# Routing the second tile of tokens first in a product-key expert layer, with its gathered rows fetched and multiplied between the pieces of the first tile's routing, and six row buffers

## The chip, the core and the metric

The kernel runs on one core of a Trainium2 chip. The core has five engines that run side by side: TensorE (PE; PEld is its weight load), VectorE (DVE), ScalarE (ACT), GpSimd (POOL) and SyncE (SP), each with an instruction queue of its own, and 16 DMA engines that all queues share. They wait for each other by semaphores. Data is worked on in the on-chip memory (SBUF, 128 partitions) and matmuls write to PSUM, eight banks. The metric is the device time of one execution in microseconds (us).

## What is computed

The program is a trunk of two layers over 256 tokens of 1024 numbers each: a mixer (matrix-memory LSTM in layer 0, differential attention in layer 1) and, after each, an expert feed-forward with 16,384 experts per layer. The change is in the feed-forward, of which this is the reference, cut:

```python
def peer_ffn(x, norm_g, w_query, sub_keys, u_table, v_table):
    h = rmsnorm(x, norm_g).reshape(T, D)                       # T = 256, D = 1024
    q = (h @ w_query).reshape(T, PEER_HEADS, 2, PEER_DHALF)    # 8 heads, two halves
    s = jnp.einsum('thpd,hpnd->thpn', q, sub_keys)             # 128 keys a half
    vals, idx = lax.top_k(s, PEER_TOPK)                        # 16 best of each half
    cand = vals[:, :, 0, :, None] + vals[:, :, 1, None, :]
    cidx = idx[:, :, 0, :, None] * N_KEYS + idx[:, :, 1, None, :]
    top_s, pos = lax.top_k(cand.reshape(T, PEER_HEADS, 256), PEER_TOPK)
    experts = jnp.take_along_axis(cidx.reshape(T, PEER_HEADS, 256), pos, axis=-1)
    gates = jax.nn.softmax(top_s, axis=-1)
    ...
        act = jax.nn.gelu(jnp.einsum('td,ted->te', hb, u_table[eb]))
        return jnp.einsum('te,ted->td', gb * act, v_table[eb])
```

So a token picks 8 x 16 = 128 experts; each has a row of u, with which the token's hidden vector is multiplied, and a row of v, which is added with the gate times the gelu of that product.

## The kernel before

All tables are float32. The feed-forward of a layer (`ffn(l)` on every engine) treats its 256 tokens in two ways.

**160 tokens (`N`) go through the whole table.** The table streams in as **units** of 512 KB: 128 up units (a unit is all 1024 numbers of 128 experts of u) and 128 down units of v. SP loads them into a ring of four buffers (`raw`, `RING`, L447), each as soon as the unit four before it is used. TensorE multiplies an up unit with the hidden vectors `h32` in 8 matmuls (`up`, L1751; the trace has 16 records a unit) and ScalarE writes the gelu to `G` (L770), two units at a time. VectorE multiplies `G` with the gates: for groups of 8 tokens it makes one-hot matrices (`one_hots`, L1276 to L1286), TensorE turns them into a 128 x 64 table of gates (`weights`, L1762) and VectorE multiplies (`weigh`, L1296); that happens from unit 64 (`HALF`) to 104 and from 128 to 168. The down units (`down`, L1811) then sum over the experts.

**The other 96 tokens are "own" tokens**, the last ones of the second tile of 128 tokens (`GT` = 64 and `GT2` = 32). Their rows are gathered: GpSimd issues an indirect DMA (`fetch`, L543) that brings 128 rows of 4 KB, one in each partition, 512 KB in all. There are 96 fetches of u rows and 96 of v rows in a layer (`FETCHES`), into a ring of four buffers (`FETCH_RING`, `fetched`). A u fetch is multiplied with the own hidden vectors on VectorE (`row_dot`, L1316, called a dot here), a v fetch is added into `own_out` (`row_add`, L1324). GpSimd issues fetch n when dot or addition n - 4 is done. VectorE goes through the units by number (the loop over `w` from `DOT_AT` = 48, `wait_ge(used, first + w)`), and `row_unit(k)` says at which unit dot or addition k stands: from unit 48 to unit 248 (`ADDED_AT`), with a gap of `GELU_GAP` units between the two kinds.

**The routing** is the top-k search, and VectorE does it by itself beside the first up units. It comes in pieces. A first-level piece (`top16`, L1182 to L1194, over 128 keys) searches four of the 16 score rows of a tile: four pieces a tile, eight in all. GpSimd then makes 80 candidate sums a head (`candidates`, L497), and a second-level piece searches four heads: two pieces a tile. The differences of the best scores go to ScalarE for the exponential (L763, at unit `EXP_AT` = 32). The rank arithmetic (L1222 to L1233) turns places among the candidates into ranks, the expansion (L1237 to L1246, once for each tile and half) turns ranks into key numbers, and L1247 makes the expert number. After the softmax (L1250 to L1252) VectorE signals `slots_ready` and `own_ready` (L1255). GpSimd spreads the expert numbers and gates of the own tokens over the partitions by six small DMAs (`own_indices`, L533) and can issue its first fetch. TensorE transposes the key numbers and gates (`slots`, L1772) ahead of unit 44 (`SLOTS_AT`), and VectorE copies them out (L1260 to L1265) and makes the first two one-hots ahead of the dots.

The order of work on an engine is the order of the code; there is no scheduler. Most of the buffers named are areas of one tensor `big` (`area`), laid out by hand so that areas which are dead by then lie over each other. `G` takes its first 20,480 columns.

## Time and profile before

| | |
|---|---|
| median of 3 runs | 1674.6 us (1673.51 to 1674.79) |
| the profiled execution | 1676.3 us, span 1674.5 us |
| TensorE busy | 1609.0 us, 96% of the span |
| VectorE busy | 1086.8 us, 65% |
| DMA | 531.89 MB, mean 318 GB/s; 241 to 410 GB/s in the slices of the feed-forward |
| the chain that ended last | TensorE 73%, DMA 20% |
| up and down matmuls | 609.4 us (L1811) and 583.1 us (L1751), 4096 records each |

The two feed-forwards are the stretches from 194 to 832 us and from 1027 to 1665 us. A busy TensorE is not a TensorE at its peak, since the ends of matmuls are modelled in the trace. What it waits for is seen better in how far apart the units stand. The granted TensorE clock is 1.00 in all the stretches shown below. In the rows by stretch, the busy time of each engine is in us, with the number of its instructions in brackets; the last three columns are the granted TensorE clock, the busy share of the DMA engines, and what they moved.

### The profile page before, as it was taken

Reading aid. Unit: us, or ns where it says so; the run is one execution under the profiler, and the core shown is the slowest. Engines: PE = TensorE matmul, PEld = TensorE weight load, DVE = VectorE, ACT = ScalarE, POOL = GpSimd, SP = SyncE. Lnnn points to the kernel's source line nnn. Section 1 sums busy time; section 2 is a strip of 40 time slices with the busy share of each in tenths; the row PEclk is TensorE's granted clock in tenths of the full one; section 3 lists DMA queues with packets and bytes.
Section 4 is the critical chain, followed back from the end, with each engine's and each line's share of the span. In section 5 each row is a group of like instructions: output and inputs, shape, how many; then the busy total and the mean of one; then the engine's idle time right before and its main releaser. Section 6 shows DMA issues by size and latency. Waiting matters only on the chain.

```text
span 1674.5 us, 30593 instructions
## 1 busy us (share of the span) xinstructions
PE 1609.0 (96%) x11542; PEld 1466.0 (88%) x11542; DVE 1086.8 (65%) x2275; ACT 296.5 (18%) x632; POOL 434.2 (26%) x457
## 2 busy tenths in 40 slices
PE   8999999999999999999999999999999999999999
PEld 6788999899988988888877789998999899888887
DVE  5588795478747864544278777954787487654552
ACT  5485411000000000000056752110000000000000
POOL 0012001234433343333000020013344332433330
PEclk9999999999999999999999999999999999999999
DMA  6546478999999999999754264789999999999995
GB/s 244 161 136 197 151 241 279 355 393 410 409 409 399 352 404 409 409 409 410 275 165 140 100 205 140 246 279 362 391 408 408 409 403 358 409 409 410 409 410 193
DMA packets 149137, 531.89 MB, mean 318 GB/s; under 512 B 16880, under 2 KB 20224, under 8 KB 148672
## 3 DMA queue, kind: packets, MB, share of 16 engines
q1 hardware_dynamic: 88416, 321.43, 51.8%
q0 software_dynamic: 56672, 204.70, 31.5%
q10 hardware_dynamic: 3968, 4.71, 1.2%
q8 instruction: 48, 0.79, 0.2%
q14 instruction: 33, 0.27, 0.0%
HBM read 527.41 MB, written 1.06 MB: 316 GB/s over the span
## 4 chain that ended last, share of the span: by engine, by line
PE 73%; DMA 20%; issue 3%; DVE 3%; ACT 1%; ACTq 0%; SPq 0%; POOL 0%; DVEq 0%
PE ps L1811 30%; PE ps L1751 21%; DMA raw<-stream 17%; PE ps L1567 4%; PE ps L1582 3%; DMA big<-u_rows,own 3%; PE ps L1584 3%; PE ps L1583 3%; PE ps L1565 2%; PE ps L1762 2%; PE ps L1739 1%; PE ps L1702 1%; PE ps L1922 1%; PE ps L1564 1%; PE ps L1892 0%
## 5 line engine op out<-in xcount | busy, mean ns | idle before, releaser
L1811 PE MATMUL ps<-big,raw 128*128 (+1 forms) x4096 | 609.4, 304 | 26.6 <-DMA raw<-stream 6.7
L1811 PEld LDWEIGHTS ps<-big,raw 128*128 128x128 f32 x4096 | 562.0, 190 | 70.8 <-issue 62.9
L1751 PE MATMUL ps<-big,raw 128*128 128x160 f32 x4096 | 583.1, 301 | 17.7 <-DMA raw<-stream 14.5
L1751 PEld LDWEIGHTS ps<-big,raw 128*128 128x128 f32 x4096 | 559.3, 190 | 36.8 <-DMA raw<-stream 18.5
L1324 DVE SCALAR_TENSOR_TENSOR big<-big,own_act 128x1024 f32<-128x1024 f32 x192 | 246.6, 1285 | 213.9 <-DMA big<-v_rows,own 209.7
L1316 DVE SCALAR_TENSOR_TENSOR big<-big 128x1024 f32<-128x1024 f32 x192 | 233.7, 1224 | 151.9 <-DMA big<-u_rows,own 104.5
L543 POOL DMA_INDIRECT big<-u_rows,own x192 | 198.8, 1035 | 335.2 <-DVE big L1316 319.2
L543 POOL DMA_INDIRECT big<-v_rows,own x192 | 193.0, 1005 | 321.5 <-DVE big L1324 305.3
L575 ACT ACTIVATE wh<-raw 128x1024 fp32r<-128x1024 f32 x97 | 102.1, 1058 | 311.1 <-DMA raw<-stream 275.6
L895 DVE TENSOR_TENSOR wl<-raw,wh 128x1024 fp32r<-128x1024 f32 x97 | 122.1, 1269 | 49.2 <-ACT wh L575 27.4
L770 ACT ACTIVATE big<-ps 128x320 f32<-128x320 f32 x128 | 56.0, 437 | 552.4 <-PE ps L1751 513.1
L1567 PE MATMUL ps<-hT,wh 128*128 128x512 f32 x280 | 100.2, 396 | 0.0
L1582 PE MATMUL ps<-wh,hT 128*128 128x512 f32 x224 | 91.5, 408 | 0.1
L1583 PE MATMUL ps<-wl,hT 128*128 128x512 f32 x224 | 87.9, 392 | 0.0
L1584 PE MATMUL ps<-wh,hT 128*128 128x512 f32 x224 | 87.9, 392 | 0.0
L1565 PE MATMUL ps<-hT,wl 128*128 128x256 f32 x320 | 83.0, 280 | 0.0
L1296 DVE SCALAR_TENSOR_TENSOR big<-ps,big 128x512 f32<-128x512 f32 x80 | 54.9, 686 | 17.3 <-PE ps L1762 13.5
L1565 PEld LDWEIGHTS ps<-hT,wl 128*128 128x128 f32 x320 | 60.3, 188 | 4.3
L1567 PEld LDWEIGHTS ps<-hT,wh 128*128 128x128 f32 x280 | 52.6, 188 | 10.3
L522 POOL DMA_DIRECT2D big<-big x12 | 6.3, 538 | 211.9 <-DVE big L888 211.9
L1281 DVE TENSOR_TENSOR hots_i<-iota_h,slot_d 128x1024 f16<-128x1024 f16 x80 | 54.8, 685 | 0.0
L1286 DVE TENSOR_TENSOR hots_j<-same_j,gate_d 128x1024 f16<-128x1024 f16 x80 | 54.8, 685 | 0.0
(250 smaller groups left out, 1057.4 us busy)
## 6 DMA issues: line engine op xcount, KB each, us to landing
raw<-stream SPq DMA_DIRECT2D x609, 512.0 KB
big<-u_rows,own POOLq DMA_INDIRECT x192
big<-v_rows,own POOLq DMA_INDIRECT x192
big<-keys ACTq DMA_DIRECT2D x2, 1024.0 KB, 7.6
big<-row_copy ACTq DMA_DIRECT2D x6, 256.0 KB, 5.4
x<-x_in SPq DMA_DIRECT2D x1, 1024.0 KB, 5.8
big<-big POOLq DMA_DIRECT2D x4, 256.0 KB, 3.4
big<-big POOLq DMA_DIRECT2D x8, 128.0 KB, 3.8
```

The source lines that it names most:

```text
L543: pool.indirect_dma_start(out=fetched[:, b, :], out_offset=None, in_=table, in_offset=bass.IndirectOffsetOnAxis(ap=own[:, 0, k:k + 1].bitc ...
L575: act.activation(wh[:, r, :], raw[:, r, :], ACT.Copy).then_inc(high_ready, 1)
L895: dve.tensor_tensor(wl[:, r, :], raw[:, r, :], wh[:, r, :].bitcast(F32), ALU.subtract).then_inc(made_low(unit), 1)
L1316: dve.scalar_tensor_tensor(out=row, in0=row, scalar=1.0, in1=own_h[k // GT], op0=ALU.mult, op1=ALU.mult, accum_out=own_act[:, k:k + 1]).th ...
L1324: dve.scalar_tensor_tensor(out=out_, in0=row, scalar=own_act[:, k:k + 1], in1=out_, op0=ALU.mult, op1=ALU.add).then_inc(row_used, 1)
L1565: pe.matmul(near, w_l[:, kd, :], hTh[:, kd, :], start=False, stop=False)
L1567: i = pe.matmul(wide, w_h[:, kd, :], hT[:, kd], start=False, stop=(kd == KD - 1))
L1582: pe.matmul(out(t), h_h, w_h[:, k, :], start=(kd == 0), stop=False)
L1583: pe.matmul(out(t), h_h, w_l[:, k, :], start=False, stop=False)
L1584: i = pe.matmul(out(t), h_l, w_h[:, k, :], start=False, stop=(kd == KD - 1))
L1751: i = pe.matmul(ps[:, r % 4, 0:N], w[:, kd, :], h32[:, kd, :], start=(kd == 0), stop=(kd == KD - 1))
L1811: i = pe.matmul(ps[:, c // 2, c % 2 * N:(c % 2 + 1) * N], w[:, c, :], g, start=(fresh_bank and c % 2 == 0), stop=last, skip_group_check=True)
```

## The change

**Order of the routing.** The scores of the second tile (t = 1) are made first, and VectorE routes that tile alone: its four first-level pieces, one piece of tile 0 (while GpSimd makes candidates), its two second-level pieces, its ranks and two expansions, and the expert numbers of the own tokens. There `own_ready` is signalled the first time, and GpSimd spreads the numbers alone (plane 0 of `own`) and begins to fetch.

**Dots between the pieces.** The rest of tile 0's routing stands in seven pieces with 20 dots between them: 2, 3, 3, 3, 3, 3 and 3. The wait for the own hidden vectors (`own_h_ready`) stands ahead of them. GpSimd makes tile 0's candidates after its first 11 fetches.

**Gates apart.** The gates of the own tokens are ready later, so `own_ready` is signalled a second time; ScalarE issues six DMAs for them at unit 64 (plane 1 of `own`, `gate_spread`), and VectorE waits for them ahead of the first addition.

**Numbers.** `FETCH_RING` 4 to 6, `EXP_AT` 32 to 44, `SLOTS_AT` 44 to 56. The slot copies and first one-hots now stand at unit 57 in VectorE's loop. `row_unit` spreads the other 172 dots and additions over the same units 48 to 248 as all 192 before. Areas of `big` are moved so that six row buffers fit.

On VectorE, the end of the last expansion and what came behind it before (L1247 makes the expert numbers; no dot stands here, the first comes behind these rows):

```order
279 L1246 TENSOR_REDUCE big<-big 128x128
280 L1247 SCALAR_TENSOR_TENSOR own_of<-big 128x128
281 L1250 TENSOR_REDUCE big<-big 128x16
282 L1251 RECIPROCAL big<-big 128x16
283 L1252 TENSOR_TENSOR big<-big 128x256
284 L1255 COPY own_of<-big 128x128
285 L1257 MEMSET big 128x1024 x2
286 L1260 CAST slot_d<-ps 128x1024
287 L1262 TENSOR_SCALAR gate_h<-ps 128x256
288 L1264 COPY gate_d<-gate_h 128x256x2
289 L1265 SCALAR_TENSOR_TENSOR gate_d<-ps,gate_h 128x256x2
290 L1276 TENSOR_TENSOR same_j<-iota_h,slot_d 128x512
```

and the same place now (L1279 makes the expert numbers, L1260 is a dot):

```order
243 L1279 SCALAR_TENSOR_TENSOR own_of<-big 128x128
244 L1190 MAX big<-big 128x8 x4
245 L1193 MAX_INDEX big<-big 128x8 x4
246 L1196 MATCH_REPLACE big<-big 128x128 x4
247 L1199 MAX big<-big 128x8 x4
248 L1202 MAX_INDEX big<-big 128x8 x4
249 L1260 SCALAR_TENSOR_TENSOR big,own_act<-big 128x1024 x2
250 L1190 MAX big<-big 128x8 x4
251 L1193 MAX_INDEX big<-big 128x8 x4
252 L1196 MATCH_REPLACE big<-big 128x128 x4
253 L1199 MAX big<-big 128x8 x4
254 L1202 MAX_INDEX big<-big 128x8 x4
```

The softmax and all that follows moved behind the dots, and three first-level pieces of tile 0 moved behind the expert numbers.

On GpSimd, from the candidates to the fetches before (L497 candidates, L533 spread, L543 fetches):

```order
23 L497 TENSOR_TENSOR big<-big 128x8x32
24 L497 TENSOR_TENSOR big<-big 128x8x16 x3
25 L497 TENSOR_TENSOR big<-big 128x8x32
26 L497 TENSOR_TENSOR big<-big 128x8x16 x3
27 L533 DMA own<-own_of 64x2x64 x2
28 L533 DMA own<-own_of 32x2x32 x4
29 L543 DMA big<-u_rows,own 128x1024 x96
```

and now (L501 candidates, L536 spread, L546 fetches):

```order
23 L501 TENSOR_TENSOR big<-big 128x8x32
24 L501 TENSOR_TENSOR big<-big 128x8x16 x3
25 L536 DMA own<-own_of 64x64 x2
26 L536 DMA own<-own_of 32x32 x4
27 L546 DMA big<-u_rows,own 128x1024 x11
28 L501 TENSOR_TENSOR big<-big 128x8x32
29 L501 TENSOR_TENSOR big<-big 128x8x16 x3
30 L546 DMA big<-u_rows,own 128x1024 x85
```

The second tile of candidates moved into the row of u fetches, and the spread carries one plane instead of two.

The core of the diff:

```diff
-FETCH_RING = 4
+FETCH_RING = 6
...
-        sc = area(28672, NT, 16, NKEYS)
-        eq = area(28672, NT, SLOTS, TOPK, dt=F16)
-        own_h = [area(26624, D), area(27648, D)]
+        sc = area(10240, NT, 16, NKEYS)
+        eq = area(18432, NT, SLOTS, TOPK, dt=F16)
+        own_h = [area(22528, D), area(23552, D)]
...
-        h32 = area(22528, KD, N)
-        fetched = area(28672, FETCH_RING, D)
+        h32 = area(20480, KD, N)
+        fetched = area(26624, FETCH_RING, D)
...
-        EXP_AT = 32
+        EXP_AT = 44
...
-        SLOTS_AT = 44
+        SLOTS_AT = 56
         DOT_AT, ADDED_AT, GELU_GAP = 48, U_E + 120, 4
+        DOTS_FIRST, DOTS_ROUTING = 5, 20
...
-            return DOT_AT + k * (ADDED_AT - GELU_GAP - DOT_AT) // (2 * FETCHES) + (GELU_GAP if k >= FETCHES else 0)
+            spread_ = (k - DOTS_ROUTING) * (ADDED_AT - GELU_GAP - DOT_AT) // (2 * FETCHES - DOTS_ROUTING)
+            return DOT_AT + spread_ + (GELU_GAP if k >= FETCHES else 0)
...
-                pool.wait_ge(own_ready, l + 1)
+                pool.wait_ge(own_ready, 2 * l + 1)
...
-                for t in range(NT):
-                    candidates(l, t)
+                candidates(l, 1)
                 own_indices(l)
                 for f in range(FETCHES):
+                    if f == DOTS_FIRST + FETCH_RING:
+                        candidates(l, 0)
                     fetch(l, (u_rows0, u_rows1)[l], f)
...
-                        act.wait_ge(own_ready, l + 1)
+                        act.wait_ge(own_ready, 2 * l + 2)
+                        for n, at_, k in ((GT, P - GT, 0), (GT2, P - GT - GT2, GT)):
+                            for g in range(P // n):
+                                act.dma_start(own[g * n:(g + 1) * n, 1, k:k + n], own_of[at_:at_ + n, 1, g * n:(g + 1) * n]
+                                              ).then_inc(gate_spread, 16)
...
+                for a in range(0, 16, 4):
+                    first16(1, a)
+                first16(0, 0)
+                second16(1, 0)
+                second16(1, 4)
+                ranks(1)
+                for s in range(2):
+                    expand(1, s)
+                dve.scalar_tensor_tensor(out=own_of[:, 0].bitcast(U32), in0=slotv[:, 0, 1], scalar=float(NKEYS),
+                                         in1=slotv[:, 1, 1], op0=ALU.mult, op1=ALU.add).then_inc(own_ready, 1)
+                dve.wait_ge(own_h_ready, 2 * (l + 1))
+                first16(0, 4)
+                dots(2)
+                first16(0, 8)
+                dots(DOTS_FIRST - 2)
+                first16(0, 12)
+                dots(3)
+                second16(0, 0)
+                dots(3)
+                second16(0, 4)
...
+                dots(3)
+                ranks(0)
                 for s in range(2):
+                    expand(0, s)
+                    dots(3)
                 dve.wait_ge(exp_ready, l + 1)
...
                 for w in range(DOT_AT, 2 * U_E):
                     dve.wait_ge(used, first + w)
+                    if w == SLOTS_AT + 1:
+                        slot_rows()
+                        one_hots(0, 0)
+                        one_hots(0, 1)
...
-                for t in range(NT):
+                for t in (1, 0):
```

Here `first16(t, a)` and `second16(t, a)` are the pieces of `top16` for tile t, `ranks(t)` and `expand(t, s)` the rank arithmetic and the expansion of one tile, `dots(n)` the next n calls of `row_dot`, and `slot_rows()` the copies of L1260 to L1265.

## Rows read from the trace of the kernel before

**Rows 1.** Stretches: length, busy PE, PEld, DVE, ACT, POOL (counts), PEclk, DMA share, GB/s.

```profile
194.00:243.00 49.00, 49.00 (x363) 49.00 (x363) 47.38 (x311) 6.89 (x14) 3.49 (x8) 1.00 0.68 226
243.00:280.00 37.00, 37.00 (x275) 37.00 (x274) 30.19 (x82) 6.68 (x12) 3.56 (x7) 1.00 0.77 243
280.00:300.00 20.00, 19.20 (x143) 18.99 (x142) 5.75 (x10) 1.75 (x4) 3.72 (x4) 1.00 0.90 326
300.00:341.00 41.00, 37.62 (x257) 34.93 (x256) 19.74 (x32) 3.50 (x8) 14.81 (x16) 1.00 0.98 378
341.00:441.00 100.00, 99.21 (x962) 97.16 (x962) 84.64 (x151) 8.76 (x20) 41.15 (x38) 1.00 1.02 403
441.00:502.00 61.00, 57.22 (x386) 52.58 (x384) 31.50 (x52) 5.24 (x12) 23.05 (x24) 1.00 1.03 409
502.00:606.00 104.00, 100.62 (x958) 96.88 (x958) 83.44 (x130) 0.72 (x2) 42.27 (x36) 1.00 0.99 380
606.00:812.00 206.00, 194.91 (x1289) 176.80 (x1288) 101.92 (x80) 0.00 (x0) 72.06 (x76) 1.00 1.02 406
...
1439.00:1644.00 205.00, 194.12 (x1280) 175.65 (x1280) 102.97 (x81) 0.00 (x0) 72.08 (x76) 1.00 1.02 406
```

**Rows 2.** TensorE in time order: start, us, engine, line, operation, tiles, shape, count.

```profile
355.92 1.10 PE L1762 MATMUL ps<-hots_j,hots_i 128*128 128x64 f16 x32
356.85 8.94 PE L1751 MATMUL ps<-big,raw 128*128 128x160 f32 x64
365.63 1.10 PE L1762 MATMUL ps<-hots_j,hots_i 128*128 128x64 f16 x32
```

**Rows 3.** The chain that ended last: start, us, what; two pieces of the down stage.

```profile
730.27 2.44 PE ps L1811 x16
732.83 2.44 PE ps L1811 x16
```

**Rows 4.** Waits: engine, line, releaser: us in total, times, longest us.

```profile
DVE big L1324 <- DMA big<-v_rows,own: 209.7, 168, 1.8
...
DVE slot_d L1260 <- PE ps L1772: 32.3, 2, 16.7
```

**Rows 5.** VectorE in order of time; in brackets idle time before, and releaser.

```profile
189.15 0.87 DVE L1182 MAX8 big<-big 128x8 f32<-128x128 f32 x4
...
194.49 0.87 DVE L1182 MAX8 big<-big 128x8 f32<-128x128 f32 x4
...
235.99 0.67 DVE L1182 MAX8 big<-big 128x8 f32<-128x80 f32 x4
...
240.34 0.67 DVE L1182 MAX8 big<-big 128x8 f32<-128x80 f32 x4
...
249.59 0.42 DVE L1222 CAST big<-big 128x512 f16<-128x512 uint32 x1
...
253.34 1.23 DVE L1237 TENSOR_TENSOR big<-big,iota_h 128x2048 f16<-128x2048 f16 x1
...
257.77 1.22 DVE L1237 TENSOR_TENSOR big<-big,iota_h 128x2048 f16<-128x2048 f16 x1
...
271.05 0.29 DVE L1247 SCALAR_TENSOR_TENSOR own_of<-big 128x128 uint32<-128x128 f32 x1
...
300.21 1.23 DVE L1316 SCALAR_TENSOR_TENSOR big<-big 128x1024 f32<-128x1024 f32 x1 [3.97 <-issue]
...
312.00 1.23 DVE L1316 SCALAR_TENSOR_TENSOR big<-big 128x1024 f32<-128x1024 f32 x1 [1.92 <-DMA big<-u_rows,own]
```

**Rows 6.** GpSimd (POOL) in order of time, same columns.

```profile
272.98 3.36 POOL L533 DMA_DIRECT2D own<-own_of  x6 [39.41 <-DVE own_of L1255]
279.80 1.04 POOL L543 DMA_INDIRECT big<-u_rows,own  x1 [3.47 <-DMA own<-own_of]
...
303.83 0.94 POOL L543 DMA_INDIRECT big<-u_rows,own  x1 [1.17 <-DVE big L1316]
```

**Rows 7.** One line's instructions: ns shortest/median/longest, first and last start.

```profile
L543 POOL DMA_INDIRECT big<-u_rows,own x192: 942/947/1971, 279.8 to 1375.4; - x192
```

More of the change, by code:

```diff
@@ L354, in program @@
         HOT_UNITS = 2 * GROUPS
+        OWN_LOADS = P // GT + P // GT2
         LO = 4
@@ L514, in _ @@
             ROW_LOADS = P // GT + P // GT2 + 1
-            OWN_LOADS = P // GT + P // GT2
             def own_rows(l):
@@ new lines, in row_landing, with row_dot @@
+                def row_landing(n):
+                    b, before = n % FETCH_RING, 2 * FETCHES * l
+                    dve.wait_ge(row_landed[b], 16 * ((before + n) // FETCH_RING + 1))
+                    return fetched[:, b, :]
+                def row_dot(k):
+                    row = row_landing(k)
+                    dve.scalar_tensor_tensor(out=row, in0=row, scalar=1.0, in1=own_h[k // GT], op0=ALU.mult, op1=ALU.mult,
+                                             accum_out=own_act[:, k:k + 1]).then_inc(row_used, 1)
@@ new lines, in ffn, with dots @@
+                rows_done = [0]
+                def dots(count):
+                    for k in range(rows_done[0], rows_done[0] + count):
+                        row_dot(k)
+                    rows_done[0] += count
+                for a in range(0, 16, 4):
[8 more added lines that the diff above has]
+                                         in1=slotv[:, 1, 1], op0=ALU.mult, op1=ALU.add).then_inc(own_ready, 1)
@@ L1733, in ffn @@
                 pe.wait_ge(loaded_keys[l], 16)
-                for t in range(NT):
+                for t in (1, 0):
                     for b in range(4):
```

130 lines of the change are left out of this document (58 added, 72 removed).

## The prediction, made before the change was run

> **What bounds the kernel now.** I read the busy times by stretch first. From the start of the up units to the first fetch (194 to 280 us) TensorE is busy all the time and DMA moves 226 to 243 GB/s; from about 341 us on DMA moves 403 to 409 GB/s until the last fetch, 380 in the stretch 502 to 606, and the second layer reads alike [rows 1]. A unit is 16 matmul records: 638 records in the first 86 us make 39.9 units of 2.16 us [rows 1]. Where rows are fetched beside them the same 16 records come every 2.56 us (730.27, 732.83) [rows 3]. In 2.56 us one unit and one fetch land, 0.524 MB each, which is 409.6 GB/s: the link is full. A load of either kind then costs 1.28 us of link, and the unit loop waits for the link, not for TensorE. VectorE agrees: in the down stage it waited 168 times for a fetched row, 209.7 us in all [rows 4]. So a layer has a link budget: 256 units and 192 fetches. What the kernel wastes of it lies before the first fetch at 279.80 [rows 6], where TensorE's 2.16 us a unit leaves 40% of the link idle.
>
> **Where fetches can start.** A piece of first-level search takes 194.49 - 189.15 = 5.34 us, one of the second level 240.34 - 235.99 = 4.35, the rank arithmetic of both tiles 253.34 - 249.59 = 3.75 (estimate for one tile 2.6, as half the width doesn't halve short instructions), one expansion 257.77 - 253.34 = 4.43 [rows 5]. Before, all of it for both tiles and the softmax stand ahead of the index spread, which POOL issues at 272.98 [rows 6]. Now VectorE needs five first-level pieces (26.7), two second-level (8.7), the ranks (2.6), two expansions (8.9) and the index product (0.3): 47.2 us from 189.15, so 236.3. The spread takes POOL 279.80 - 272.98 = 6.8 us as before [rows 6], with half the bytes, so the first fetch is issued at about **243** instead of 280.
>
> **Is VectorE done in time?** It gets 20 dots of 1.23 us [rows 5], 24.6 us, and 1.5 us for the split ranks. At 241.6 (the sixth piece) it comes to dot 0, and the row isn't there: the fetch issued at 303.83 [rows 6] was the one that released the dot at 312.00 [rows 5], 8.2 us, so row 0 is due at 251.3 and the wait is 9.7 us. Walking the later batches with rows landing 2.56 us apart and a new fetch after each dot, I find each row landed before its dot or under 2 us after. POOL now makes tile 0's candidates ahead of fetch 11; behind them only fetches queue, and with up to six rows out they are covered. Before, routing took 83.5 us (189.15 to 272.7); now 83.5 + 24.6 + 1.5 + 9.7 = 119.3, end at about **308.5**. TensorE asks for the slots at unit 56, which by the next part starts at about 325: 17 us of cover. Before, VectorE waited up to 16.7 us for these transposes [rows 4], so the cover is the same size. ScalarE stops at unit 44 (about 296) for the differences, which VectorE hands over ahead of its last nine dots, at about 284. ScalarE's six new DMA issues cost at most 3.36 us (POOL's price for six [rows 6]) at an engine busy 8.76 of 100 us [rows 1]: nothing. The slot copy moved behind unit 57 has seven units of time; nothing.
>
> **The rest of the first 48 units.** By 243, 22.6 units have run. Up to unit 48 the link carries 25.4 units, less about two already landed ahead, and about 23 fetches: 46.4 loads, 24.3 MB. At 409.6 GB/s that is 59.4 us; at the 326 GB/s of the stretch where four fetches started before, 74.6; at the 378 of the next stretch [rows 1], 64. I take 63, as the fetches here don't pause for 17 us as they did. Unit 48 then starts at 306, before at 300 (the dot of 300.21 [rows 5] waits for it): **+6 us**, ends +2.5 and +18.
>
> **After unit 48.** Before, from 300.2 to the last fetches at about 811.5 (unit 248; 606 to 812 has 1289 records, 80.6 units [rows 1]), 200 units and 188 fetches: 203.4 MB in 511.3 us, 398 GB/s. Now 200 units and 169 fetches, 193.5 MB: 486.3 us at the same rate, -25.0. Two stretches give less. Where weights are built a group of four units takes 365.63 - 355.92 = 9.71 us even when nothing is late [rows 2], 2.43 a unit, over 80 of the 200 units, just above the link's 1.28 x (1 + 172/196) = 2.40. And 502 to 606 moved only 380 GB/s [rows 1], so waits other than the link's count there: of its 5 us share I leave out half. That makes -22.5. The far end is the full link in the other 120 units: 120 x 2.40 + 80 x 2.43 = 483, -28.5.
>
> **Sum.** Per layer +6 - 22.5 = -16.5 (ends -26 and -4.5); both layers **-33 us**. The tail behind unit 248 is untouched. The profiled execution has a span of 1674.5 and 1676.3 us in all, 1.7 over the median of 1674.6; against the median the forecast is **1641.6 us**.
>
> **A rule against it.** 192 u-row fetch issues took 942 to 1971 ns, median 947 [rows 7], though VectorE was busy 84.6 of the 100 us from 341 [rows 1]; so a fetch issue loses at most 1.0 us to VectorE, and at 1.97 us it still fits into the 2.56 us in which a row lands. The Trainium skill (SBUF — State Buffer, "SBUF: two separate sides") has the trap that VectorE instructions which take both ports keep GpSimd from writing its DMA descriptors until they end; casts, copies and tensor_scalar are named. By that rule fetches issued beside ranks and casts would wait an instruction each, and the sum would stay; the longer form of it is the last rival.
>
> **Rivals.**
> 1. *The link starts fuller than I say.* For: 409 GB/s is held for 60 us on end (441 to 502) [rows 1]. Against: it took from 280 to past 341 to get there. Both layers at the far ends: 2 x -26, **1623 us**. Chance 0.12.
> 2. *A slow start.* With few fetches out the link moved 326, then 378 GB/s [rows 1]; if the interleaved ones, six at most and drained between pieces, do no better, unit 48 comes at 318 and a layer gains 4.5 to 11: **1653 to 1666 us**. For: 8.2 us from issue to use. Against: six buffers, and 20 dots bunched two or three at a time keep several out. Chance 0.16.
> 3. *It doesn't do what it says.* The early rows aren't multiplied early because their index or the gained hidden rows come late, and the dots only move: **1672 to 1678 us**. Against: the hidden rows are asked for after the index, and POOL has nothing else to do then. Chance 0.04.
> 4. *Slower: routing ends too late.* If each of the six later batches of dots waits a whole 8.2 us (say, since fetch issues are held until a VectorE piece ends, which is the rule above carried over to the searches), VectorE is 49 us later, at 358. TensorE stops at unit 56 for the 32 us beyond its cover, from which it decides; what a layer gains is 16.5, so it loses 16: **1706 us**. Break-even is 33 us of lateness. Against: the issue times of [rows 7]. Chance 0.06.
>
> The forecast itself (1632 to 1652) has 0.62. The range 1624 to 1662 takes in part of the first two rivals and leaves out about 0.17. Faster by over 0.2% (about what a measurement of this kernel can tell from no change): 0.62 + 0.12 + 0.16 = 0.90; within it 0.04; slower 0.06.
>
> **What the new profile would show.** First fetch issued near 243 and about 1077; units from 243 to 306 at 2.3 to 2.6 us with DMA near 385 GB/s; 16 records every 2.56 us only now and then after unit 104, on average 2.40 to 2.44; VectorE's waits for v rows well under 209.7 us; no wait of TensorE for the slots. Wrong would be: ScalarE or TensorE idle for VectorE around units 44 to 64 (rival 4), under 360 GB/s from 250 to 300 (rival 2), or unit times of 2.56 in the down stage with fewer fetches in them, which would mean that something other than the shared link sets 2.56.

## The result

| | median, us | runs | against the kernel before |
|---|---|---|---|
| before | 1674.6 | 5, 1672.4 to 1676.6 | |
| changed | 1663.65 | 5, 1659.0 to 1667.0 | ratio 0.9934, 95% interval 0.9920 to 0.9948 |

The change gains 11 us, where 33 were forecast; the time lies above the range. Further runs of the same file (e8_after_again, below) gave 1662.7 and a ratio of 0.9928.

The profiled execution of the changed kernel has a span of 1665.2 us. Its groups of instructions (line, engine, operation, tiles, count, then busy us and mean ns, then idle time ahead of them with what ended most of it) show three things at once. TensorE idles ahead of both unit loops for loads of units. VectorE's additions no longer wait for v rows, but for TensorE, whose units they are timed by. And the chain that ended last has a quarter of its time in unit loads:

```profile
PE 68%; DMA 26%; issue 2%; DVE 2%; ACT 1%; SPq 0%; ACTq 0%; DVEq 0%; another core or an unknown queue 0%
PE ps L1853 26%; DMA raw<-stream 25%; PE ps L1793 21%; PE ps L1609 4%; PE ps L1624 3%; PE ps L1626 3%; PE ps L1625 3%; PE ps L1607 2%; PE ps L1804 1%; PE ps L1781 1%; PE ps L1744 1%; PE ps L1606 1%; PE ps L1934 0%; PE ps L1964 0%; ACT big L596 0%
...
L1853 PE MATMUL ps<-big,raw 128*128 (+1 forms) x4096 | 593.3, 303 | 24.6 <-DMA raw<-stream 16.9
L1793 PE MATMUL ps<-big,raw 128*128 128x160 f32 x4096 | 587.3, 302 | 29.1 <-DMA raw<-stream 23.8
...
L1365 DVE SCALAR_TENSOR_TENSOR big<-big,own_act 128x1024 f32<-128x1024 f32 x192 | 246.4, 1283 | 214.9 <-PE ps L1853 202.9
```

The stretches of layer 0, cut at units 0, 22.5, 39, 48, 64, 104, 128, 168 and 248 of the changed kernel (length, busy time of PE, PEld, DVE, ACT, POOL with counts, granted clock, DMA share, GB/s), answer to [rows 1]:

```profile
192.00:241.00 49.00, 49.00 (x364) 49.00 (x363) 45.80 (x249) 6.89 (x14) 5.48 (x11) 1.00 0.68 227
241.00:280.00 39.00, 34.70 (x239) 32.40 (x238) 30.39 (x139) 3.06 (x7) 21.85 (x21) 1.00 0.99 375
280.00:306.00 26.00, 25.05 (x173) 23.38 (x171) 25.04 (x56) 5.37 (x9) 11.08 (x9) 1.00 1.02 403
306.00:346.00 40.00, 37.29 (x263) 35.54 (x262) 25.10 (x42) 3.50 (x8) 17.51 (x14) 1.00 0.98 386
346.00:448.00 102.00, 100.07 (x964) 97.32 (x964) 81.23 (x145) 8.74 (x20) 38.38 (x37) 1.00 1.01 392
448.00:509.00 61.00, 56.41 (x390) 52.97 (x389) 29.31 (x49) 5.68 (x13) 22.62 (x23) 1.00 1.02 401
509.00:610.00 101.00, 99.46 (x965) 97.36 (x964) 78.78 (x112) 0.28 (x1) 37.55 (x30) 1.00 0.97 368
610.00:809.00 199.00, 188.28 (x1280) 175.13 (x1280) 89.53 (x70) 0.00 (x0) 63.87 (x65) 1.00 1.00 388
```

The reader is to see that DMA now moves 375 to 403 GB/s at once from 241 us on, as forecast, and that it moves *less* than before further on: 388 GB/s in the down stage, where [rows 1] has 406. With the start of each unit taken as every 16th matmul record of the two unit loops, both kernels divide so (us; the two layers):

| units | before | changed |
|---|---|---|
| 0 to 24 | 52.2, 52.2 | 52.2, 52.2 |
| 24 to 48 | 53.9, 54.1 | 61.8, 61.6 |
| 48 to 64 | 41.2, 41.3 | 40.2, 38.8 |
| 64 to 104 | 99.8, 100.9 | 101.7, 104.2 |
| 104 to 128 | 61.3, 62.1 | 60.5, 59.7 |
| 128 to 168 | 104.2, 101.5 | 100.8, 99.4 |
| 168 to 248 | 205.1, 205.3 | 199.3, 198.7 |
| 48 to 248 | 511.6, 511.2 | 502.5, 500.7 |

So a layer loses 7.5 to 7.9 us ahead of unit 48 (forecast: 6) and wins 9.1 to 10.5 behind it (forecast: 22.5). Ahead of unit 48 all went as told; behind it more than half of the gain is missing, though 22 fetches a layer are gone from there (GpSimd issues 188 in units 48 to 248 before, 166 now). From its first unit to its last a layer gains 1.1 and 2.9 us in these two profiles (7.7 and nothing in the second profile of the changed kernel, e8_after_again). The other 5 us by which the two spans differ lie ahead of the first unit (192.1 us against 193.9) and between the layers (193.1 against 196.5), which the change doesn't touch. Over the profiles of all kernels below that left these parts alone they scatter from 191.2 to 194.4 and from 193.1 to 196.5 us, so a single profile carries some 3 us of chance at each place, and the gain of 11 us is that of the medians.

### The profile page after: what moved, and what is told of

It is laid out like the page before. It is cut to its first block, busy times and chain, and to the rows that moved or that the text cites. A ratio compares the mean times of both kernels' runs of the same rounds, so it can differ in the third digit from the quotient of the medians.

```text
span 1665.2 us, 30651 instructions
## 1 busy us (share of the span) xinstructions
PE 1592.1 (96%) x11542; PEld 1461.7 (88%) x11542; DVE 1087.6 (65%) x2293; ACT 296.3 (18%) x632; POOL 459.4 (28%) x457
## 4 chain that ended last, share of the span: by engine, by line
PE 68%; DMA 26%; issue 2%; DVE 2%; ACT 1%; SPq 0%; ACTq 0%; DVEq 0%; another core or an unknown queue 0%
PE ps L1853 26%; DMA raw<-stream 25%; PE ps L1793 21%; PE ps L1609 4%; PE ps L1624 3%; PE ps L1626 3%; PE ps L1625 3%; PE ps L1607 2%; PE ps L1804 1%; PE ps L1781 1%; PE ps L1744 1%; PE ps L1606 1%; PE ps L1934 0%; PE ps L1964 0%; ACT big L596 0%
## 5 line engine op out<-in xcount | busy, mean ns | idle before, releaser
L1853 PE MATMUL ps<-big,raw 128*128 (+1 forms) x4096 | 593.3, 303 | 24.6 <-DMA raw<-stream 16.9
L546 POOL DMA_INDIRECT big<-v_rows,own x192 | 203.8, 1062 | 366.8 <-DVE big L1365 333.1
L1260 DVE SCALAR_TENSOR_TENSOR big<-big 128x1024 f32<-128x1024 f32 x192 | 231.1, 1226 | 107.6 <-PE ps L1793 77.2
L546 POOL DMA_INDIRECT big<-u_rows,own x192 | 210.1, 1094 | 312.5 <-DVE big L1260 282.8
```

The source lines that it names most:

```text
L546: pool.indirect_dma_start(out=fetched[:, b, :], out_offset=None, in_=table, in_offset=bass.IndirectOffsetOnAxis(ap=own[:, 0, k:k + 1].bitc ...
L1260: dve.scalar_tensor_tensor(out=row, in0=row, scalar=1.0, in1=own_h[k // GT], op0=ALU.mult, op1=ALU.mult, accum_out=own_act[:, k:k + 1]).th ...
L1853: i = pe.matmul(ps[:, c // 2, c % 2 * N:(c % 2 + 1) * N], w[:, c, :], g, start=(fresh_bank and c % 2 == 0), stop=last, skip_group_check=True)
```

## The experiments

Times are medians; "before" beside them is the kernel before on the same chip, 1673.2 to 1674.7 us each time. The forecast's premise is called the link budget: a load of either kind costs 1.28 us of a full link.

### What is a fetch worth?

e1_84 and e1_48: the kernel before with fewer fetches (own rows left out of the output, as the expectations say).

```diff
-FETCHES = SLOTS * (GT + GT2) // P
+OWN_ROWS = SLOTS * (GT + GT2) // P
+FETCHES = 84
...
-        own = sb("own", [P, 2, FETCHES])
+        own = sb("own", [P, 2, OWN_ROWS])
```

> The kernel before with 84 + 84 fetches a layer in place of 96 + 96, spread over the same units 48 to 248; the last 12 rows of each kind of the own tokens are left out. Link budget (the prediction's theory: each load costs 1.28 us of a full link): units 48 to 248 fall from 511 us to TensorE's floor of 483, 28 us a layer, 1618 us in all. Half share (a unit beside a fetch takes 2.56 us, one without takes TensorE's own 2.17, or 2.43 where weights are built, so a fetch costs 0.39 or 0.13 us wherever it stands): 24 fetches less give 7 us a layer, 1660 us.

> The kernel before with 48 + 48 fetches a layer; half of the own tokens' rows are left out. Link budget: the link has room for all 96 fetches beside units at TensorE's floor, so units 48 to 248 take 120 x 2.17 + 80 x 2.43 = 455 us, 56 less a layer, 1563 us. Half share: 96 fetches less at 0.39 (60% of them) or 0.13 us give 28 us a layer, 1619 us.

Measured: 1649.2 us with 84 + 84 (ratio 0.9843, 0.9824 to 0.9861) and 1626.3 us with 48 + 48 (0.9724, 0.9709 to 0.9740). The link budget asked for 1618 and 1563, the half share for 1660 and 1619; both missed both. Against the 1673.2 us of the kernel before on this chip, a fetch that is taken out gives back 0.50 us (48 fetches, 24 us), and 0.24 us if four times as many go (192 fetches, 47 us in all), not 1.28. And it is not the link that keeps TensorE: with 48 + 48 it moves 318 GB/s in the down stage, where the kernel before has 406, and still the chain that ended last (start, us, what) runs through unit loads that take 6.8 to 8.0 us:

```profile
639.27 8.03 DMA raw<-stream
...
650.05 6.79 DMA raw<-stream
...
664.88 6.84 DMA raw<-stream
```

In the ring of four, a unit is asked for when the unit four places ahead of it has been used, so that it has three units of time to land. At TensorE's own pace (52.2 us for 24 units) that is 6.5 us. From the issues and landings of the traces: with nothing beside it, as in units 8 to 40 of the kernel before, a unit load takes 3.9 us on average and is never late. In units 170 to 247 of the kernel before it takes 7.5 us and is nearly always late; of the changed kernel 7.0 us, late two times in three; with 48 + 48 fetches 6.0 us, late one time in five. An average under 6.5 does not help where the ring can't hold more than three units in advance: what one late unit costs is not made up by the next that come early. That is the ring theory. The runs below test it.

### The parts of the change

e2_ring4: the changed kernel, `FETCH_RING = 4`. e3_ring6: the kernel before with six buffers and the changed kernel's areas. e4_dense: the changed kernel with the additions planned to end 20 units earlier.

```diff
-        DOT_AT, ADDED_AT, GELU_GAP = 48, U_E + 120, 4
+        DOT_AT, ADDED_AT, GELU_GAP = 48, U_E + 100, 4
```

> The changed kernel with four row buffers in place of six (tile 0's candidates then stand behind nine fetches). Half share: no difference, 1664 us within 3, as the fetches are the same in number. If the six buffers let fetches bunch and starve the unit stream, four are faster by 5 us or more. If six are needed to keep the link full while VectorE routes, four are slower by 5 us or more.

> The kernel before, order of routing and dots as it was, with six row buffers and the areas of the changed kernel. Half share: no difference to the kernel before, 1674.6 us within 3. If the 11 us that the change brought come from the buffers, this shows them: about 1664 us. If the four were what kept a full link in the down stage, six keep it as well, since VectorE waits there for rows.

> The changed kernel with its 172 later dots and additions packed into units 48 to 228 in place of 48 to 248: one fetch beside nearly every unit, then 20 units with none. Half share: the price of a fetch doesn't depend on where it stands, so 180 x 2.56 + 20 x 2.17 = 504 us for units 48 to 248 as against 502 now: no difference within 4 us. Link budget: the same loads on a link that is full to unit 228 and 60% busy behind it, so that 20 units at 2.17 lose 17 us of link time a layer: if the changed kernel were held by the budget this would be slower by up to 10 us a layer.

Measured: 1659.2 us (0.9905, 0.9889 to 0.9921), 1679.3 us (1.0033, 1.0020 to 1.0046), 1676.1 us (1.0019, 1.0009 to 1.0029). The order of the routing brings the gain, and the two added buffers none: in the order of before they and the moved areas cost 5 to 6 us, which none of the expectations had, in the new order they seem to cost 3 to 4 (the runs of the changed kernel and of e2_ring4 overlap). The ring theory would explain the cost, since each unit load then has more beside it, but that is an argument and was not measured. e4_dense loses 13 us to the changed kernel, which the half share ruled out (4 us at most) and the link budget allowed; see the last set.

e8_after_again: the changed kernel itself, beside the runs of the next set.

> The changed kernel once more, with a second profile, beside the others on this chip. The first profile had 9.3 us less span than the profile before, but only 4 of it inside the two feed-forwards (635.1 and 633.2 us from first to last unit against 636.2 and 636.1). If 4 us is the gain of the change and the rest is scatter of the mixers, the feed-forwards read 633 to 635 us again and the time is 1664 to 1672 us; if the scatter lies in the feed-forwards they differ by more.

Measured: 1662.7 us (0.9928, 0.9904 to 0.9951).

### Does the queue's share make a unit load slow?

e6_twoq_before, e7_twoq_after: every second unit load from ScalarE's queue, the rest from SP's as before (shown is ScalarE's part, which comes behind each pair of gelus).

```diff
                     act.wait_ge(used, first + 2 * pair + 2)
+                    load_after(first + 2 * pair + 1)
```

> The kernel before, with every second unit of the up and down stream loaded by ScalarE's queue in place of SyncE's (same ring of four, same moment, after the same wait). Nothing else differs; the gelu of the own tokens' products moves behind ScalarE's load of unit 150. If the DMA engines serve queues in turn, the unit stream gets two shares of three while a fetch is out: a unit then needs 1.92 us of link, less than TensorE's 2.17, and fetches get what is left, 168 GB/s, one every 3.1 us. The cost of a fetch to the units goes to nearly nothing, but 192 fetches at one a unit no longer fit, so VectorE's waits for rows set the pace in the down stage: a gain of 0 to 15 us a layer, and units of 2.17 us up to where the rows run late. If 2.56 us comes from something else than shares of queues (latency of a ring of four, or the link as such), nothing changes: 1674 us.

> The changed kernel with the same two queues for the unit stream. By turns between queues the early fetches no longer slow the units, so units 24 to 48 go back from 61.7 to about 54 us, the link stays full with units first, and the 20 early dots are a gain: each fetch that is out of the way early saves link time later. 10 to 25 us a layer under the changed kernel, 1615 to 1645 us, and more below it than e6 is below the kernel before. Otherwise 1664 us.

Measured: 1681.7 us (1.0049, 1.0033 to 1.0065) and 1677.5 us (1.0043, 1.0011 to 1.0074), 8 and 15 us slower than the kernels they start from on this chip. In their profiles the stage from the first to the last unit is about as long as there (632.3 and 633.8 us for e7_twoq_after; 635.9 and 640.7 for e6_twoq_before, whose second layer takes 29.4 us for its last eight units instead of 21.0), and 4 to 8 us are lost between the layers. The rest of the 15 us stays open: the profiled execution of e7_twoq_after took 1673.1 us, 4 less than the median. The bytes did go over two queues (e6_twoq_before; q1 and q10 carry the units):

```profile
q0 software_dynamic: 56672, 204.70, 31.7%
q1 hardware_dynamic: 51840, 188.24, 30.4%
q10 hardware_dynamic: 40544, 137.89, 21.7%
```

The queue-share theory fell. It isn't that ScalarE, between its gelus, asked too late: its loads go out within 0.2 us of the end of the unit that frees their buffer, and in units 170 to 247 of e6_twoq_before a unit load lands 7.0 us behind its issue on either queue. The Trainium skill (DMA: Bandwidth & Descriptors, "Rules for kernel authors") says that spreading transfers over SP, ScalarE and GpSimd gives no bandwidth; these two runs agree.

### A deeper ring, at few fetches

e9_48_two is the control, 48 + 48 fetches with two fetch buffers; e10_48_eight has eight unit buffers in the freed room: units 0 to 3 of each eight go to `raw`, units 4 to 7 to four areas that are free in this stage, and a unit is asked for seven units ahead.

```diff
-                        sp.wait_ge(used, RING * turn + (unit + 1))
-                        sp.dma_start(raw[:, r, :],
-                                     stream[bass.ds(RING * turn + (unit + RING), 1)].rearrange("a p f -> (a p) f")
-                                     ).then_inc(landed[r], 16)
+                        to, done = (raw[:, r, :], landed[r]) if k < RING else (extra[r], landed_w[r])
+                        sp.wait_ge(used, 8 * turn + (unit + 1))
+                        sp.dma_start(to, stream[bass.ds(8 * turn + (unit + 8), 1)].rearrange("a p f -> (a p) f")
+                                     ).then_inc(done, 16)
```

> The order of the kernel before with 48 + 48 fetches a layer instead of 96 + 96 (the other own rows are left out of the output, as in the run with 48 + 48 that stands at 1626.3 us), two fetch buffers instead of four, and the score and comparison areas where the changed kernel has them. It is the control of the next run: the two freed buffers make room for four more unit buffers there. Both theories expect what four buffers gave, 1615 to 1640 us: a fetch is asked for only every 5 us here.

> The same with eight unit buffers instead of four: a unit of the experts' weights may be asked for seven units ahead, not three. Theory now (a unit load beside fetches takes 5.7 to 7.5 us from issue to landing, three units of TensorE's own pace are 6.5 us, and the ring of four cannot bank more): the units run at TensorE's own pace, units 48 to 248 in 455 to 465 us instead of about 488, and the kernel gains 45 to 65 us on its control. Rival (a fetch slows the unit itself, by a quarter to half a microsecond, whatever is banked): no change, within 5 us of the control. The link budget of the prediction has nothing to say here, since 296 loads would fill the link for 379 of 488 us only.

Measured: 1627.5 us and 1556.7 us, that is 71 us for four buffers of 512 KB (ratios to before 0.9722 and 0.9303, intervals of 0.003 to either side). The stretch of units 168 to 248, in the same columns as above, first of the control, then with eight:

```profile
594.00:788.00 194.00, 179.50 (x1281) 174.32 (x1280) 50.10 (x39) 0.00 (x0) 34.97 (x37) 1.00 0.91 320
```

```profile
578.00:752.00 174.00, 174.00 (x1283) 174.00 (x1283) 49.56 (x39) 0.00 (x0) 35.09 (x37) 1.00 0.97 356
```

The same units and fetches in 174 us instead of 194, TensorE busy all of it. The waits (engine, line, releaser: us in total, times, longest) of the control begin with these two; with eight buffers no wait of TensorE for a load is left in the list:

```profile
PE ps L1812 <- DMA raw<-stream: 31.0, 42, 1.6
PE ps L1752 <- DMA raw<-stream: 15.6, 23, 1.8
```

and the chain that ended last, between 600 and 760 us, is one piece of it:

```profile
599.98 160.15 PE ps L1833 x1179
```

Units 48 to 248 take 455.0 us in both layers (control 490.4 and 487.6). The rival, that a fetch slows the unit itself, fell: 48 fetches a stage cost TensorE nothing once its loads are asked for early enough. 455 us is also the pace of a layer when nothing is late: 2.175 us a unit, 2.43 where weights are built.

e11_two and e12_two_eight: all 96 + 96 fetches, two fetch buffers, ring of four and of eight.

> The kernel before with two fetch buffers instead of four and the score and comparison areas of the changed kernel, all 96 + 96 fetches. Control of the next run. If a fetched row takes 5 to 8 us from issue to its use, two in flight bring one every 2.5 to 4 us where 2.7 are wanted: 1675 to 1780 us, VectorE and through it TensorE late for rows rather than for units.

> The same with eight unit buffers. Ring theory: TensorE no longer waits for units, but the 392 loads between unit 48 and unit 248 fill the link at 409.6 GB/s for 502 us, so it is 10 to 40 us faster than its control unless the two fetch buffers set its time, and not under 1655 us. Rival (the fetch slows the unit itself): as the control, within 5 us.

Measured: 2116.1 us and 2083.2 us. Two buffers are far too few, more so than expected, and VectorE waits for rows all along (first line e11_two, then e12_two_eight):

```profile
DVE big L1324 <- DMA big<-v_rows,own: 445.0, 181, 7.1
```

```profile
DVE big L1340 <- DMA big<-v_rows,own: 433.9, 184, 5.7
```

The pair says little of the question asked, since the fetches set its time in units 64 to 104 and 128 to 168 (158 to 175 us for 40 units). Elsewhere it agrees: units 168 to 248 take 190 us with four unit buffers and 173.9 with eight.

### A deeper ring, at all fetches

Room for four more unit buffers beside four fetch buffers comes from moving the scores, candidates and ranks, and from letting `own_out` take `own_h`'s place once the dots are done. e13_eight_before has the order of before, e14_eight_after that of the changed kernel, e16_layout_after is the control: the changed kernel with the same areas and the ring of four. The ring's diff is that of e10_48_eight; with it comes

```diff
-        own_out = [area(24576, D), area(25600, D)]
+        own_out = own_h
...
+                    dve.wait_ge(row_used, 2 * FETCHES * l + FETCHES)
+                    for c in range(2):
+                        dve.memset(own_out[c], 0.0).then_inc(own_zero, 1)
                     dve.wait_ge(own_zero, 2 * (l + 1))
```

> The kernel before, all 96 + 96 fetches and four fetch buffers, with eight unit buffers. Room for the four new ones comes from moved areas (scores, candidates, ranks) and from own_out taking own_h's place once the dots are done, so that its two memsets stand between dots and additions. If the ring of four unit buffers is what keeps the link below full, the unit loop now really waits for the link: 392 loads of 1.28 us between unit 48 and unit 248 are 502 us (before 511), and the stretch 24 to 48 loses its last waits: 1650 to 1662 us. If the link itself gives no more than the 398 GB/s it moved, 1670 to 1678.

> The changed kernel with four fetch buffers (as in the run that stands at 1659.2 us) and eight unit buffers, room made in the same way. If the ring was why the prediction's step on the units after 48 failed, that step now holds: 369 loads of 1.28 us are 472 us against the measured 502, units 24 to 48 lose 2 to 4 us of their 61, and the kernel takes 1590 to 1615 us; against the order of before with eight buffers it gains 33 us or more. If a fetch slows the unit itself, 1655 to 1665.

> The control of the run before it: the same areas, four fetch buffers, own_out in own_h's place, and the ring of four unit buffers as it was. Both theories expect the 1659 us that the changed kernel takes with four fetch buffers, 1652 to 1668; the two memsets between dots and additions cost 1 to 2 us of VectorE, no more.

| | ring | median, us | ratio to before | units 24 to 48 | 48 to 248 |
|---|---|---|---|---|---|
| before | 4 | 1674.7 | | 53.9, 54.1 | 511.6, 511.2 |
| e13_eight_before | 8 | 1649.2 | 0.9843 (0.9817 to 0.9869) | 52.8, 52.8 | 499.6, 500.4 |
| e16_layout_after | 4 | 1656.9 | 0.9888 (0.9855 to 0.9922) | 59.4, 59.4 | 497.9, 499.2 |
| e14_eight_after | 8 | 1620.6 | 0.9674 (0.9647 to 0.9702) | 52.2, 52.2 | 489.2, 486.5 |

The deeper ring gives 25 us in the old order and 36 in the new. The order gives 28.6 us with eight buffers (33 forecast), and 18 with four. (The order of before has no run with these areas and the ring of four, so its 25 us hold what the areas do as well; in the new order the areas alone make 2 us, 1659.2 against 1656.9.) e14_eight_after stayed 6 us above its expected range. Its stretches of units 64 to 104, 104 to 128, 128 to 168 and 168 to 248 show, from the second on, the full link that the forecast took for given:

```profile
333.00:445.00 112.00, 100.52 (x959) 99.79 (x960) 93.22 (x167) 8.31 (x19) 46.65 (x41) 0.94 0.98 380
445.00:497.00 52.00, 52.00 (x385) 52.00 (x384) 25.62 (x42) 5.24 (x12) 18.18 (x21) 1.00 1.03 409
497.00:595.00 98.00, 97.77 (x962) 96.78 (x961) 80.74 (x115) 0.72 (x2) 38.82 (x33) 1.00 1.02 405
595.00:785.00 190.00, 184.54 (x1284) 175.21 (x1283) 91.93 (x73) 0.00 (x0) 63.76 (x68) 1.00 1.03 409
```

and its waits (both layers) name what is late next: VectorE waits for rows, and hands TensorE the material of the expert weights late.

```profile
DVE big L1278 <- DMA big<-u_rows,own: 127.7, 85, 6.9
...
DVE big L1381 <- DMA big<-v_rows,own: 124.7, 100, 2.0
```

```profile
PE ps L1828 <- DVE hots_j L1355: 23.9, 4, 10.1
...
PE ps L1877 <- DMA raw<-stream: 2.4, 4, 1.1
```

The first of the four stretches takes 112 us where 97 are possible, at 380 GB/s, and that in both layers: more than the 6 us that the expectation missed. TensorE in order of time shows where they go in layer 0, and the second fence the granted clock (third column from the end) just then:

```profile
338.28 4.59 PE L1817 MATMUL ps<-big,raw 128*128 128x160 f32 x32
...
356.45 1.03 PE L1828 MATMUL ps<-hots_j,hots_i 128*128 128x64 f16 x16 [9.23 <-DVE hots_j L1355]
359.73 1.03 PE L1828 MATMUL ps<-hots_j,hots_i 128*128 128x64 f16 x16 [2.25 <-DVE hots_j L1355]
360.58 7.07 PE L1817 MATMUL ps<-big 128*128 128x160 f32 x32
```

```profile
352.00:365.70 13.70, 7.00 (x51) 6.85 (x52) 12.75 (x23) 0.00 (x0) 6.74 (x6) 0.50 0.71 250
```

TensorE stands idle for 9.23 and 2.25 us until VectorE, late by its rows, hands over the one-hots. Within the first wait its granted clock falls to 0.50, the lower level of 1.2 GHz, and stays there for 13.7 us; two units take 7.07 us then instead of 4.59. The 7.0 us of work at half speed cost 3.5 us (an estimate), which with the two waits makes the 15 us.

The down stage holds a warning for whoever reads rings from traces. In its units 170 to 247 a unit load of e14_eight_after takes 14.8 us from issue to landing, about the 15.2 us that seven units allow, and half of the loads are late again, at 409 GB/s. On a full link a load here grew as long as the ring let it; with 48 + 48 fetches and the same ring (e10_48_eight) it took 6.1 us. So the 7.5 us of the kernel before would have been seen with a full link alone, too; it is the runs with few fetches that show the ring.

### Where the fetches end

e17_eight_dense, e18_eight_110, e19_eight_late: e14_eight_after with `ADDED_AT` at `U_E + 100`, `U_E + 110` and `U_E + 126` instead of `U_E + 120`, so that the last row is added about unit 228, 238 and 254.

> The changed kernel with four fetch buffers and eight unit buffers (1620.6 us) and the additions planned to end at unit 228 instead of 248, as in the run with the ring of four that this cost some 12 us. If the pace of the fetches mattered there only because three units of advance could not bridge a bunch of fetches, it matters no more: 1615 to 1626 us. If bunching costs by itself, through VectorE or the link, the same 12 us again: 1630 to 1637.

> The same with the additions planned to end at unit 238. By the first theory 1615 to 1624 us; by the second half the loss, about 1626.

> The changed kernel with four fetch buffers and eight unit buffers, the additions planned to end at unit 254 instead of 248 (1620.6 us). Theory after the two denser runs (1636.1 at unit 238, 1649.0 at unit 228): with eight buffers the link is the bound, and units behind the last fetch leave 2.17 - 1.28 = 0.9 us of it idle each, 9 us for ten units in each layer, which is what the denser runs lost (15 and 28 us in two layers). Six units later then gains up to 5 us a layer, less what the additions delay at the end: 1610 to 1619 us. Rival (denser runs lost time because rows and weights crowd on VectorE in units 64 to 104 and 128 to 168): the fewer rows there gain 1 to 3 us a layer too, and the end of the loop shows no gain; the stretches tell.

Measured: 1649.0 us (0.9850, 0.9827 to 0.9873), 1636.1 us (0.9780, 0.9761 to 0.9799) and 1618.3 us (0.9670, 0.9638 to 0.9703). Both theories of the first two expectations missed: the loss of 28 us is larger than with the ring of four. The last 20 units before 248 show what the link then leaves unused, first of e17_eight_dense, then of e14_eight_after:

```profile
756.00:800.00 44.00, 43.62 (x317) 42.92 (x317) 5.22 (x5) 0.00 (x0) 0.94 (x1) 1.00 0.87 314
```

```profile
738.00:785.00 47.00, 45.88 (x321) 43.58 (x320) 21.84 (x17) 0.00 (x0) 12.65 (x14) 1.00 1.03 410
```

Behind the last fetch TensorE's own pace leaves 2.17 - 1.28 = 0.9 us of link idle in each unit, which would be 18 us a layer for 20 units and 9 for ten. The rows show less, 314 of 409 GB/s over 44 us, or 10 us; the difference would fit a ring that fills up again there. Measured from the first to the last unit, e17_eight_dense is 12.5 and 17.3 us a layer longer than e14_eight_after, and e18_eight_110 5.8 and 7.6. The time isn't lost at the end itself: units 168 to 248 take 189.9 and 189.5 us in e17_eight_dense, 189.8 and 189.9 in e14_eight_after. It is lost in units 48 to 168, where the 9 and 11 fetches more than in e14_eight_after now stand: 12.3 and 17.6 us, most of it in units 128 to 168 (106.2 and 108.6 us instead of 98.0 and 97.1, at 405 and 400 GB/s). So a fetch that moves there costs 1.4 to 1.6 us, what the link budget has or somewhat more. Part of that is the clock: e17_eight_dense is at its lower level for 6.8 and 10.2 us more than e14_eight_after, which can cost up to half of these (an estimate). That rows and weights also crowd on VectorE there, the rival of the last expectation, is not excluded in units 64 to 104, where both kernels stay at 380 to 385 GB/s; in e19_eight_late, most of the gain stands in units 168 to 248 (186.5 and 186.9 us), as the link budget wants it. Moving the end back six units shortens the layers by 4.6 and 2.0 us in the profiles, while the medians differ by 2.3 us, less than their intervals: within its expected range, and not shown to be faster. The two fastest kernels of the study, e14_eight_after and e19_eight_late, beat the changed kernel by 43 to 45 us. Of e4_dense's 13 us the same reasoning could explain all, but how they divide was not measured.

## Why the prediction was wrong

- **First fetch at 243.** Right. GpSimd in order of time (start, us, engine, line, operation; idle before and releaser), to be held against [rows 6]:

```profile
234.65 3.12 POOL L536 DMA_DIRECT2D own<-own_of  x6 [24.19 <-DVE own_of L1279]
240.32 1.03 POOL L546 DMA_INDIRECT big<-u_rows,own  x1 [2.55 <-DMA own<-own_of]
```

  In the second layer the first fetch came at 1069.1 instead of 1077. Counted in pieces the index was due at 236.3 and came at 234.3; from spread to fetch 5.7 us instead of 6.8, with half the bytes.
- **The first dot waits 9.7 us.** Of the right kind, smaller: 6.3 us, as row 0 landed 5.5 us behind its issue and not 8.2.

```profile
245.84 1.23 DVE L1260 SCALAR_TENSOR_TENSOR big<-big 128x1024 f32<-128x1024 f32 x1 [6.28 <-DMA big<-u_rows,own]
```

- **VectorE ends the routing at 308.5.** Right: the gates of the second tile, its last piece ahead of the memsets, are at 305.2 us. TensorE didn't wait for the slots. VectorE stood idle for 4.67 us ahead of their copy, released by a unit's matmuls: it was ahead of TensorE and waited for unit 57, where the copy stands:

```profile
329.43 1.23 DVE L1313 CAST slot_d<-ps 128x1024 f16<-128x1024 f32 x1 [4.67 <-PE ps L1793]
```

- **Unit 48 comes 6 us later.** Nearly: 7.5 to 7.9 us, and with eight unit buffers nothing: units 24 to 48 take 52.2 us with the change and 52.8 without it. So most of this cost isn't the link's either: TensorE waited for loads that the ring asked for too late. The size came out near for a reason that the forecast didn't give: it took 63 us from the rates of two stretches in which the same ring was at work. That is luck in part.
- **After unit 48, 486 us at the rate of before: -22.5 us.** This is the step that failed: 9.1 and 10.5 us. Its ground was "a load of either kind then costs 1.28 us of link, and the unit loop waits for the link, not for TensorE", read from units of 2.56 us at 409.6 GB/s [rows 1, 3]. In the kernel before two limits stood at the same place, as the 25 us that the deeper ring gives in the old order show. The link was full, since VectorE was always behind with its rows and so kept its fetch buffers in flight [rows 4]; and each unit load took 7.5 us, about three units of 2.56. Taking fetches away frees the first limit and hardly the second. In the changed kernel loads still took 7.0 us on average, where the ring allows 6.5 at TensorE's own pace. The 22 fetches gave back 0.4 to 0.5 us each, about as the 48 of e1_84 did, and not 1.28. Pieces of the chain at 690 to 760 us:

```profile
701.77 8.46 DMA raw<-stream
...
720.13 7.01 DMA raw<-stream
...
735.01 7.38 DMA raw<-stream
...
759.74 8.11 DMA raw<-stream
```

  The rate of 398 GB/s wasn't kept but fell to 388 in the down stage and 368 in the stretch of the second weights. The last sentence of the forecast's signs named this outcome ("something other than the shared link sets 2.56"), but gave it no rival and no price; units of the down stage came every 2.49 us, between its 2.56 and the 2.40 to 2.44 expected. The trace of before held a hint: alone its unit loads landed 3.9 us behind their issue, beside fetches 7.5 us, and 6.5 was what the ring could bear. It was no proof, since a full link makes loads long as well.
- **The premise with the ring taken away.** With eight unit buffers the same order gives 28.6 us, near the 33 of the sum, but its terms are not those of the sum: units 24 to 48 lose nothing instead of 6 us a layer, and units 48 to 248 gain 10.4 and 13.9 us instead of 22.5. Four fetch buffers get fewer fetches out ahead of unit 48, so only 13 or 14 are gone from behind it, at 0.8 to 1.0 us each. With the ring of four and the same areas (e16_layout_after) units 48 to 248 gain 13.7 and 12.0 us on the kernel before, for 18 and 17 fetches, 0.7 to 0.8 us each. So the deeper ring took away the cost ahead of unit 48 and raised the worth of a fetch a little; it did not bring the 22.5 us back, and that the total comes near 33 is in part luck.
- **The rivals.** Rival 2 had the right time (1653 to 1666) by the wrong mechanism: it wanted unit 48 at 318 us and under 360 GB/s from 250 to 300; unit 48 came at 306, and 375 to 403 were moved. Rival 1 fell. Rival 3 fell, as the rows are multiplied where the change says. Rival 4 fell: neither ScalarE nor TensorE waited for VectorE between units 44 and 64. Issues of u fetches took 946 ns in the median and 1993 at most, as in [rows 7], and 1094 ns on average against 1035 before, so the rule of the two ports cost them next to nothing more than there.
- **Six buffers.** The forecast counted them as a help against rival 2. They cost 5 to 6 us in the old order (with their areas), and brought nothing in the new.

What stays open is how the 12 to 13 us a layer that are missing behind unit 48 divide between the ring and the rest, and why a unit load takes so long beside fetches. That it shares a full link explains 7.5 us in the kernel before; with 48 + 48 fetches the link moves 320 GB/s in the down stage and single loads still take 8 us. That two queues don't help rules out the number of queues, not the order in which transfers are served.

## What to carry to other kernels

A ring's depth has to be held against the time of a load *beside everything else that is in flight*, not alone: while the link has room, depth minus one units of computing must exceed it, or each late load is lost time and removing traffic gives little back. A link that reads full does not prove that the link alone is the bound, and a load as long as the ring allows does not prove that the ring is, since both look the same on a full link. What tells them apart is a run with less traffic: if the awaited loads are still late there, try a deeper ring before a finer order. Once the ring is deep enough, the budget of the link comes close to holding, and then traffic belongs as evenly as possible over the whole stage, its start and its end.

## What else the runs showed of the chip

- A 512 KB load takes 3.9 us from issue to landing with up to two more of its kind in flight, 6.0 us beside 48 fetches of each kind a layer, 7.5 us beside 96, all with a ring of four; with a ring of eight it takes 6.1 us beside 48 and about 15 us beside 96 (units 170 to 247).
- GpSimd's four candidate additions of one tile took 1.74 us in the kernel before and 4.60 us here, beside VectorE's dots; two of those dots took 1.64 and 1.42 us instead of 1.22:

```profile
264.92 4.60 POOL L501 TENSOR_TENSOR big<-big 128x256 f32<-128x256 f32 x4 [3.15 <-DVE big L1202]
```

```profile
265.88 1.64 DVE L1260 SCALAR_TENSOR_TENSOR big<-big 128x1024 f32<-128x1024 f32 x1
...
267.46 1.42 DVE L1260 SCALAR_TENSOR_TENSOR big<-big 128x1024 f32<-128x1024 f32 x1
```

- Where TensorE waited often and long, its granted clock fell: in the run with two fetch buffers to 0.82 in the first weights stretch, where it was busy for 112 of 167 us, a mean between its levels of 1.2 and 2.4 GHz; in the down stage, busy for 184 of 194 us, it is back at 1.00, the upper one.

```profile
339.00:506.00 167.00, 112.08 (x965) 109.13 (x965) 92.80 (x162) 8.75 (x20) 41.45 (x43) 0.82 0.78 264
...
736.00:930.00 194.00, 183.67 (x1306) 177.83 (x1305) 55.16 (x44) 0.00 (x0) 39.83 (x42) 1.00 0.93 334
```
